# One product for the latent keys of two heads, in a hybrid-attention kernel on one core

## The reference, cut to what matters

```python
def mla_kv(zckv, zkr, g, w_ukv, tabs):
    kv = (rms_norm(zckv, g) @ w_ukv).reshape(B, L, MLA_HEADS, MLA_NOPE + MLA_V)   # 6 heads, 64 + 64 columns
    k_nope, v = jnp.split(kv, [MLA_NOPE], axis=-1)
    k = jnp.concatenate([k_nope, jnp.broadcast_to(k_pe, ...)], axis=-1)           # 64 + 32 columns
    return k, v
```

## Time and profile before

| | us |
|---|---|
| runs of the kernel before | 977.23, 981.51, 982.66 (median 981.51) |
| the profiled execution, device time | 978.77 |
| its span in the trace | 976.8 |
| PE busy in the span | 925.4 (95%) |
| DVE, POOL, ACT busy | 561.8, 508.5, 426.5 |
| mean granted TensorE clock | 0.979 of full speed |

### The profile page before, as it was taken

How to read it: one execution, slowest core, us unless ns; L and a number is a source line. 1 busy time by engine, 2 the same in 40 slices (tenths; PEclk the granted TensorE clock), 3 DMA queues, 4 the chain that set the end, 5 groups by cost and what they waited for, 6 DMA issues and landing times.

```text
span 976.8 us, 13266 instructions
## 1 busy us (share of the span) xinstructions
PE 925.4 (95%) x4607; PEld 661.1 (68%) x4607; DVE 561.8 (58%) x877; ACT 426.5 (44%) x873; POOL 508.5 (52%) x429
## 2 busy tenths in 40 slices
PE   4699999999999999999999889999999999999996
PEld 2378876789845666666677679888894555565584
DVE  4426615333587668973317856767247757884336
ACT  2512212423455556655433853235335645565432
POOL 2125524324497635666446427655528875566672
PEclk9699999999999999999999989999999999999998
DMA  9955454213532310020254212323243220010252
GB/s 358 340 187 194 150 190 142 74 33 81 133 82 62 79 24 18 17 66 1 82 190 138 87 30 73 87 62 101 69 106 89 62 53 18 17 54 29 76 182 87
DMA packets 44569, 95.84 MB, mean 98 GB/s; under 512 B 9500, under 2 KB 16504, under 8 KB 42456
## 3 DMA queue, kind: packets, MB, share of 16 engines
q1 hardware_dynamic: 44504, 95.00, 31.3%
HBM read 71.33 MB, written 4.21 MB: 77 GB/s over the span
## 4 chain that ended last, share of the span: by engine, by line
PE 81%; DVE 7%; ACT 4%; DMA 3%; POOL 2%; issue 2%; SPq 1%; POOLq 0%; ACTq 0%; DVEq 0%
PE banks L949 15%; PE banks L951 14%; PE banks L950 14%; PE banks L1184 12%; PE banks L1206 11%; PE banks L1159 6%; DMA area_g<-in_w_ada_dram 2%; PE banks L960 2%; PE banks L1225 2%; PE banks L1218 1%; DVE negmax L2091 1%; PE banks L1057 1%; PE banks L1321 1%; ACT late_bias L1697 1%; DMA w_raw<-in_w_out_dram 1%
## 5 line engine op out<-in xcount | busy, mean ns | idle before, releaser
L1816 POOL TENSOR_TENSOR w_split<-w_raw,w_split 128x512 fp32r<-128x512 f32 (+4 forms) x121 | 146.0, 1213 | 228.7 <-ACT w_split L1448 228.7
L949 PE MATMUL banks<-w_split,area_a 128*128 128x512 f32 (+3 forms) x606 | 230.6, 381 | 10.6 <-DVE area_a L2301 6.6
L951 PE MATMUL banks<-w_split,area_a 128*128 128x512 f32 (+3 forms) x606 | 223.4, 369 | 0.0
L950 PE MATMUL banks<-w_split,area_a 128*128 128x512 f32 (+3 forms) x606 | 222.9, 368 | 0.0
L2091 DVE TENSOR_REDUCE negmax<-banks 128x1 f32<-128x768 f32 x160 | 149.3, 952 | 80.0 <-PE banks L1159 79.6
L1448 ACT ACTIVATE w_split<-w_raw 128x512 fp32r<-128x512 f32 (+4 forms) x121 | 68.4, 580 | 204.1 <-PE banks L951 197.8
L1556 ACT ACTIVATE area_z<-banks 128x512 f32<-128x512 f32 x196 | 108.8, 598 | 79.8 <-PE banks L1184 76.4
L949 PEld LDWEIGHTS banks<-w_split,area_a 128*128 128x128 f32 x606 | 114.9, 190 | 41.9 <-issue 20.7
L1184 PE MATMUL banks<-area_a 97*128 97x512 f32 (+4 forms) x448 | 129.1, 399 | 4.4 <-ACT area_z L1556 3.1
L951 PEld LDWEIGHTS banks<-w_split,area_a 128*128 128x128 f32 x606 | 114.8, 189 | 16.7
L950 PEld LDWEIGHTS banks<-w_split,area_a 128*128 128x128 f32 x606 | 115.2, 190 | 13.0
(11 more groups left out here) (209 smaller groups left out, 1460.6 us busy)
## 6 DMA issues: line engine op xcount, KB each, us to landing
area_g<-in_w_ada_dram SPq DMA_DIRECT2D x16, 1024.0 KB, 5.2
w_raw<-in_w_in_dram SPq DMA_DIRECT2D x32, 512.0 KB, 3.7
area_g<-in_w_ada_dram SPq DMA_DIRECT2D x16, 512.0 KB, 4.8
w_raw<-in_w_out_dram SPq DMA_DIRECT2D x16, 512.0 KB, 4.3
area_a<-parts SPq DMA_DIRECT2D x72, 96.0 KB, 2.1
area_a<-parts SPq DMA_DIRECT2D x30, 192.0 KB, 3.6
area_b<-in_x_dram SPq DMA_DIRECT2D x8, 512.0 KB, 9.2
w_raw<-in_w_in_dram SPq DMA_DIRECT2D x8, 352.0 KB, 3.9
```

The lines of the kernel that those rows point to most:

```text
L949: nc.tensor.matmul(dst, a[0], b[0], start=first, stop=False)
L950: nc.tensor.matmul(dst, a[0], b[1], start=False, stop=False)
L951: return nc.tensor.matmul(dst, a[1], b[0], start=False, stop=last)
L1816: op = nc.gpsimd.tensor_tensor(lo, raw, hi.bitcast(F32), ALU.subtract)
```

## The change

`w_ukv` is stored, when it is split, with the 64 key columns of all six heads first (columns 0 to 383) and the value columns behind them (384 to 767). So the key columns of two neighbouring heads lie side by side, 128 in all. The even unit's `mla_head` makes only queries; the odd unit's makes its own queries and, in one product, the keys of both heads. That product's result has the even head's key in rows 0 to 63 and the odd head's in rows 64 to 127. ACT copies each half to its head's place in `qk_t`, with one more instruction per key part, the second of them from partitions 64 to 127 to partitions 0 to 63. The split of `w_ukv` becomes two instructions on ACT and two on POOL, and `mla_values` reads 384 columns that lie together.

```diff
-def mla_parts(L):
-    return [("q", 1), ("k", 1)] + ([("q", 0)] if L < DEPTH - 1 else []) + [("k", 0)]
+def mla_parts(L, u):
+    groups = (1, 0) if L < DEPTH - 1 else (1,)
+    if u % 2 == 0:
+        return [("q", g) for g in groups]
+    return [("q", 1), ("k", 1)] + [("q", g) for g in groups[1:]] + [("k", 0)]
...
             if kind == "ukv":
-                return [(flat[:, 0:768], ukv[:, 0, :], ukv[:, 1, :])]
+                src = flat[:, 0:768].rearrange("p (h z n) -> p z h n", h=6, z=2)
+                hi, lo = (ukv[:, i, :].rearrange("p (z h n) -> p z h n", z=2, h=6) for i in range(2))
+                return [(src[:, z], hi[:, z], lo[:, z]) for z in range(2)]
...
-                v = [ukv[:, i, :].rearrange("p (h n) -> p h n", h=6)[:, :, 64:128] for i in range(2)]
+                v = [ukv[:, i, 384:768] for i in range(2)]
...
-                        mm = three(dst, [ukv[:, i, h * P:(h + 1) * P] for i in range(2)],
+                        mm = three(dst, [ukv[:, i, (h - 1) * 64:(h + 1) * 64] for i in range(2)],
                                    [cmp_t[:, 4 + i, tokens(g)] for i in range(2)])
...
                     act.wait_ge(ring_filled, r + 1)
-                    copy(qk_t[0:rows, 2 * (m % 2) + (what == "k"), tokens(g)],
-                         banks[0:rows, r % NRING, 0:len(GROUPS[g]) * P]).then_inc(ring_free, 1)
+                    if what == "q":
+                        op = copy(qk_t[:, 2 * (m % 2), tokens(g)], src)
+                    else:
+                        copy(qk_t[0:64, 2 * ((m - 1) % 2) + 1, tokens(g)], src[0:64])
+                        op = copy(qk_t[0:64, 2 * (m % 2) + 1, tokens(g)], src[64:128])
+                    op.then_inc(ring_free, 1)
...
             def mla_high(L, u):
                 m = N_MLA[L, u]
                 act.wait_ge(mla_roped, m)
+                if u % 2 == 0:
+                    act.wait_ge(ring_free, N_RING_FREE["mla", L, u + 1, mla_parts(L, u + 1)[-1]])
```

More of the change, by code:

```diff
@@ L373 @@
         if head_pair(_p + 3):
-            RING += [("mla", _L, 2 * _p + 6, part) for part in mla_parts(_L)]
+            RING += [("mla", _L, 2 * _p + 6, part) for part in mla_parts(_L, 2 * _p + 6)]
         if now:
@@ L379 @@
         if head_pair(_p + 3):
-            RING += [("mla", _L, 2 * _p + 7, part) for part in mla_parts(_L)]
+            RING += [("mla", _L, 2 * _p + 7, part) for part in mla_parts(_L, 2 * _p + 7)]
         if now and ctx:
@@ L620, in operands_free @@
             elif u == 19:
-                eng.wait_ge(ring_filled, N_RINGB["mla", L, 19, mla_parts(L)[-1]])
+                eng.wait_ge(ring_filled, N_RINGB["mla", L, 19, mla_parts(L, 19)[-1]])
             else:
@@ L937, in w_slot_ready @@
             if s[0] == "out" and s[2] == 0 and s[3] < NW:
-                eng.wait_ge(ring_filled, N_RINGB["mla", s[1], NUNIT - 1, mla_parts(s[1])[-1]])
+                eng.wait_ge(ring_filled, N_RINGB["mla", s[1], NUNIT - 1, mla_parts(s[1], NUNIT - 1)[-1]])
         PASSES = {"gqa": [(2, 0, 128), (3, 1, 65)], "diff": [(2, 0, 97)], "mla": [(2, 0, 97), (2, 1, 96), (3, 0, 96)]}
@@ L1114, in mla_head @@
                 pe.wait_ge(w_lo, N_SLICE["uq", L, 1, 0])
-                for part in mla_parts(L):
+                for part in mla_parts(L, u):
                     what, g = part
@@ L1510, in mla_copy @@
                     act.wait_ge(split_lo, N_SPLIT[L, "gqa2"])
-                for part in mla_parts(L):
+                for part in mla_parts(L, u):
                     r = N_RINGB["mla", L, u, part] - 1
                     what, g = part
-                    rows = P if what == "q" else 64
+                    src = banks[:, r % NRING, 0:len(GROUPS[g]) * P]
                     act.wait_ge(ring_filled, r + 1)
-                    copy(qk_t[0:rows, 2 * (m % 2) + (what == "k"), tokens(g)],
-                         banks[0:rows, r % NRING, 0:len(GROUPS[g]) * P]).then_inc(ring_free, 1)
+                    if what == "q":
[4 more added lines that the diff above has]
+                    op.then_inc(ring_free, 1)
             def mla_high(L, u):
@@ L2097, in mla_rope @@
                 q = qk_t[:, 2 * (m % 2), lat]
-                dve.wait_ge(ring_free, N_RING_FREE["mla", L, u, mla_parts(L)[-1]])
+                dve.wait_ge(ring_free, N_RING_FREE["mla", L, u, mla_parts(L, u)[-1]])
                 nc.vector.tensor_tensor(scr[64:96, 0, :], q[96:128], rt[96:128, :], ALU.mult)
```

## The result

The changed kernel takes 972.04 us (median of 5 runs, 969.98 to 972.93) where the kernel before, run beside it, takes 981.51 us (5 runs, 977.23 to 982.66). The ratio of the two is 0.9915 with a 95% interval of 0.9891 to 0.9938: about 8.3 us faster (9.5 by the medians), where 4.9 were forecast (975.2). In the two profiled executions the spans are 969.6 and 976.8 us, 7.2 us apart.

What follows compares the result with a forecast made beforehand. PE, busy for 95% of the span, was taken as the bound. Gains of 3 x 1.06 + 0.46 + 0.54 + 0.74 = 4.9 us, set against a middle of 980.1, gave 975.2 us; range 970.8 to 980.6.

Steps and rivals of the forecast that it cites:

- The removed matmuls: Even units' key products on PE: 0.70 and 0.36 us, together 1.06 us a period, 6.4 us over six as upper end.
- The copies on ACT: Key copies moved to the odd unit: ACT up to 0.97 us later, covered by idle time, costed at nothing; uncovered 5.8 us.
- the ring: PE's result banks, two uses fewer per period: no new wait; bounds zero and about 0.1 us a period at score step 5.
- the split: Splitting ukv by two instructions each on POOL and ACT, in chunk 4's projection: cost zero, at most 0.5 us over both layers.
- DVE's late read: PE waits at max tile 3 for DVE's tile 1 read, leaving 0.46, 0.54 and 0.74 of 1.06 us in three periods.
- Carried to the end unchanged: Behind p = 6, through the first layer's transition and to the end: the 4.9 us gain is carried whole.
- The whole 6.4: Rival: at p = 5 and 6 DVE packs closer or PE's waits are made up; 6.4 us gained, 973.7 us; chance 0.18.
- DVE's pace: Rival: DVE holds PE at p = 5 and 6, only the p = 4 periods gain, 2.1 us: 978.0 us; chance 0.20.
- Doesn't pay: Rival: the odd unit's longer ACT copies lose their cover, giving back 0.97 us a period: 980 us; chance 0.10.
- slower, by the clock: Rival: added PE waits cost one more clock fall of 1.32 us in each of eight places: 985.8 us; chance 0.06.

Runs made afterwards that it cites:

- copies_twice: Changed kernel with four unread 64 x 256 copies on ACT ahead of each odd unit's key copies; 972.48 us, ratio 0.9935.
- copies_late: Changed kernel with twelve unread 64 x 256 copies on ACT ahead of each odd unit's key copies; 988.15 us, ratio 1.0110.
- tile1_first: Changed kernel with DVE reading max tile 1 in front of the odd unit's mla_low instead of behind it; 973.02 us, ratio 0.9941.
- dead_matmuls: Changed kernel with the removed key matmuls computed again in the even unit, into a bank its query product overwrites; 978.62 us, ratio 0.9994.
- before again: The kernel before, unchanged, executed and traced once more; 978.92 us, ratio 1.0001.
- sum_first_before: The kernel before with POOL's first sum of pair 1 in the second layer held back until DVE's sums are done; 976.46 us, ratio 0.9974.
- dead_early: Changed kernel with 21 unread matmuls added, seven each at p = 2, 3 and 4 of the first layer; 975.27 us, ratio 0.9974.
- tile1_first_before: The kernel before with DVE reading max tile 1 in front of the odd unit's mla_low; 978.54 us, ratio 1.0003.
- after again: The changed kernel, unaltered, executed and traced once more; 971.23 us, ratio 0.9912.
- sum_first: Changed kernel with POOL's first sum of pair 1 in the second layer held back until DVE's sums are done; 971.12 us, ratio 0.9922.

## Why the prediction was right, and where it was not

**The removed matmuls: right.** 0.70 and 0.36 us a period were the price. At p = 4 the periods gained 1.06 and, less what other traces of before gain there, 1.17; put back, the matmuls took the gain with them.

**The copies on ACT, the ring, the split: right at nothing, the ring only in sum.** `copies_twice` shows that cover is left, `copies_late` that it has an end. The crossing copy costs what the others cost (594 ns in the mean over both kinds). One thing I had not seen: before had a short wait of scores step 4 for a key copy, which is gone. In the second layer, p = 5, that pair of scores took from 832.76 to 833.59 = 0.83 us before and from 825.88 to 826.36 = 0.48 us after:

```profile
825.88 0.63 PE L1189 MATMUL banks<-area_a 97*128 97x512 f32 x2
826.36 0.51 PE L1164 MATMUL banks<-area_a 96*128 96x384 f32 x2
826.79 0.98 PE L1189 MATMUL banks<-area_a 97*128 97x512 f32 x2
827.82 0.58 PE L1164 MATMUL banks<-area_a 96*128 96x384 f32 x2
```

But the wait has only moved to step 5, which took 833.95 to 834.42 = 0.47 us before. In `tile1_first`, where DVE's read doesn't hold the max tile behind it, step 5 takes 827.19 to 828.02 = 0.83 us, and `dead_matmuls` has 0.47 and 0.83 for the two steps. It is the place that the prediction bounded by 0.1 us, where step 5 comes close to the exponent of step 4: it costs 0.36 us there and at p = 6, and the unforeseen gain at step 4 pays for it. The bound was too small, and that the two cancel is luck.

**DVE's late read takes part back: right, and one place more.** Forecast 0.46 and 0.54 in the first layer, measured 0.43 and 0.52; forecast 0.74 at p = 6 of the second, measured 0.73. With the read in front, the two in the first layer became 1.14 and 1.04. At p = 5 of the second layer I counted the full 1.06, from DVE's 2.29 us of idle time. Most of that idle time was there only because PE had just run at the lower clock and was late: before again, at full clock, has 0.62 us ahead of its read at 832.05. Less than the 1.06 by which PE comes earlier, it is used up, and the rows above show PE's fourth group start at 827.82, which is 0.14 us behind the end of this read:

```profile
826.74 2.67 DVE L2102 TENSOR_REDUCE negmax<-banks 128x1 f32<-128x768 f32 x3
```

826.74 + 0.94 = 827.68; DVE then reads tiles 2 and 3 without a gap. Against before again and `sum_first_before`, whose clock was full there too, the period gained 0.65 to 0.68; with the read in front (`tile1_first`) it gained 2.36 - 1.44 = 0.92, so that the read costs about 0.25 of the missing 0.4 and the rest is the moved wait. The terms as measured are 1.06, 0.43, 0.52, 1.17, 0.68 and 0.73, together 4.6 us, where 4.9 were forecast.

**"Carried to the end unchanged": the step that was mis-sized.** The prediction took the rest of the kernel as shifted rigidly. By the table the span shrank by 2.4 us more than forecast, and by the measured ratio the time by 3.4. Of these
- 1.6 us are the clock of the earlier trace rows, shown by before again, which gains 1.44 and 0.16 there with no change made. The prediction priced a fall at 1.32 us and asked only whether there would be more of them, never whether the one of before would go. Whether the change made it go or the execution profiled happened to lack it stays open;
- 1.1 us, less the 0.1 to 0.2 of other executions, lie between the layers. There ACT waits for the output weights 7.81 us before and 6.56 us after:

```profile
517.59 1.15 ACT L1448 ACTIVATE cmp_t<-w_raw 128x512 fp32r<-128x512 f32 x2 [7.81 <-DMA w_raw<-in_w_out_dram]
```

```profile
514.37 1.16 ACT L1453 ACTIVATE cmp_t<-w_raw 128x512 fp32r<-128x512 f32 x2 [6.56 <-DMA w_raw<-in_w_out_dram]
```

The wait is 6.5 to 6.7 us in the six traces that reach this place about as early as after does, 7.4 in `dead_early` and 7.0 in `copies_late`, which come later, and 7.6 to 8.3 in all with the old work. On PE it shows as a wait of 0.72 us for POOL's part of that split, which after doesn't have. It goes with the time at which the work arrives, and why the transfer lands sooner stays open;
- the rest, about 1 us between the spans' 7.2 and the ratio's 8.3, is the spread of the kernel before. Its profiled execution of 978.77 lies under its median of 981.51. `sum_first_before` shows that its slower executions go when POOL is held back from DVE's sum. That these have the sum at 6.5 us rather than 3.6 is inferred, from that run and from the trace of `tile1_first`: no execution of before above 980 us was profiled. In the two that were, the sum took 3.6 and 0.8 us, which is worth 0.6 us.

**The rivals.** "The whole 6.4" named 973.7 us, nearer to the measured 972.04 than the forecast of 975.2, but by chance: its mechanism is refuted by the waits for DVE. So is "DVE's pace": p = 5 and 6 gained in either layer, and DVE still idles ahead of max tile 4 there (0.16 to 1.63 us). "Doesn't pay" and "slower, by the clock" needed more than the change brings, and `copies_late` shows both. The two falls that the prediction counts in the trace of before are not all: between the layers, behind 6.55 us of idle time of PE, the clock is 0.70 from 564.3 to 574.3 us. After has that stretch too (0.71), so the sum doesn't change.

## What to carry to other kernels

A removed instruction on the bounding engine is worth its start-to-start distance, less the lateness of the next buffer's reader, and both could be read off the trace to about a tenth of a microsecond at five of the six places here; but idle time that stands right behind a stretch at a lower clock is slack only in part (2.29 us there, 0.62 at full clock). Before a gain of half a per cent is forecast, the spread of the kernel itself wants an explanation, since a change can win or lose more by the phase into which it shifts two engines than by what it removes. And a freed microsecond is kept only if the next join of two engines is not held by a third: reading max tile 1 first paid nothing alone and some 2.5 us once POOL was kept off DVE's sum.

## What the runs showed of the hardware

An addition on DVE with two inputs in SBUF, 0.68 us undisturbed, lasted 3.6 and 6.45 us while POOL ran additions of about 1.25 us without a gap. In these three traces it did not slip in between two of them and ended only when POOL had stopped: POOL's run ended at 746.96 + 2.48 = 749.44 before, at 746.44 after, and at 745.23 in `tile1_first`, and DVE's pair of sums at 750.60, 747.59 and 746.38, each 1.15 or 1.16 us later, the first of the two some 0.55 us after POOL's end. The rows of DVE and POOL in after:

```profile
743.39 4.20 DVE L2137 TENSOR_TENSOR w_raw<-w_raw,late_bias 128x512 f32<-128x512 f32 x2
...
743.93 2.51 POOL L1875 TENSOR_TENSOR w_raw<-area_z 128x512 f32<-128x512 f32 x2
747.58 2.51 POOL L1875 TENSOR_TENSOR w_raw<-w_raw,area_z 128x512 f32<-128x512 f32 x2 [1.14 <-ACT area_z L1567]
```

In four other traces (before again, `dead_early`, `tile1_first_before`, `copies_late`) DVE did get in behind the POOL instruction that was running: its pair of sums took 2.5 to 2.6 us and POOL's next two instructions 3.3 to 3.4 in place of 2.5 (in before again DVE from 746.78 for 2.56 us, POOL from 747.10 for 3.39). In these four DVE's sum starts 0.88 to 1.00 us after that POOL instruction, which lasts 1.3 us (746.78 against 745.84 here); in the seven traces in which it loses, 0.28 to 0.80 us after it. So one program, before and before again, falls on either side by 0.3 us. That the start decides is inferred from these eleven traces, and no run set it on purpose.

The Trainium skill's page "SBUF — State Buffer", section "SBUF: two separate sides", says that the shared port pair is locked for a whole instruction by whichever engine starts first, a DVE instruction with two SBUF inputs being one that needs it against a GpSimd instruction that reads SBUF, as POOL's additions do here. The traces agree that DVE is blocked and not merely slowed, since its end follows POOL's, and show that it can lose to several POOL instructions in a row.

TensorE's granted clock fell to mostly its lower level (1.2 of 2.4 GHz) for some 3 us near 827 us in four of six traces with the old work, at the cost of 1.6 to 1.7 us each (the table's stretches of p = 4 and 5, beside before again), with the same program in one trace and not in the other (before and before again). The waits for DVE that the change adds at four places (0.45 and 0.24 us where the timeline marks them) brought no such fall in the five traces that have them (after, after again, `dead_early`, `copies_twice`, `sum_first`); waits of up to 2.4 us came with three falls in `copies_late`.
